# Gated attention with per-head states padded to 128 rows, a gate product over 128 rows, and level products of both halves placed together

## What is computed

```python
q = g_q.reshape(B, S, 4, 64) * 64 ** -0.5;  k = g_k...;  v = g_v.reshape(B, S, 4, 128)
log_a = log_sigmoid(g_a @ w_gate_up + b_gate) / 16       # g_a has 16 columns
# over chunks:
o_inter = einsum('bhcd,bhde->bhce', q * exp(b), state)   # b: running sum of log_a
o_intra = (q k^T with decay, causal) @ v
state = exp(b_last) * state + einsum('bhcd,bhce->bhde', k * exp(b_last - b), v)
```

## Time and profile before

| | us |
|---|---|
| median of 3 runs | 4049.37 (4048.47 to 4050.02) |
| span of the profiled execution | 4047.2 |
| PE busy | 4001.6 |
| DVE busy | 2201.4 |
| ACT busy | 1474.3 |
| POOL busy | 107.8 |
| GLA of layer 0 (gate to last norm product), from the span's start | 173 to 388 |
| GLA of layer 1 | 1430 to 1644 |

### The profile page before, as it was taken

How to read it: one execution, slowest core, us unless ns; L and a number is a source line. 1 busy time by engine, 2 the same in 40 slices (tenths; PEclk the granted TensorE clock), 3 DMA queues, 4 the chain that set the end, 5 groups by cost and what they waited for, 6 DMA issues and landing times.

```text
span 4047.2 us, 47426 instructions
## 1 busy us (share of the span) xinstructions
PE 4001.6 (99%) x18802; PEld 3076.8 (76%) x18802; DVE 2201.4 (54%) x3449; ACT 1474.3 (36%) x2422; POOL 107.8 (3%) x172
## 2 busy tenths in 40 slices
PE   9999999999999999999999999999999999999998
PEld 6777657888888877656888888777777777887786
DVE  7877677434434655566634334543546363646664
ACT  5434464211212433555412122333434343324533
POOL 2000000000000000000000000000000000000000
PEclk9999999999999999999999999999999999999999
DMA  7534101333332221201222221231111111116542
GB/s 263 193 109 141 40 11 32 99 94 104 94 99 83 90 67 48 76 6 37 63 88 89 78 68 47 73 110 47 37 47 44 40 47 63 42 54 227 187 160 80
DMA packets 99622, 342.13 MB, mean 85 GB/s; under 512 B 11016, under 2 KB 12072, under 8 KB 98250
## 3 DMA queue, kind: packets, MB, share of 16 engines
q1 hardware_dynamic: 78522, 258.87, 19.7%
q0 software_dynamic: 20880, 80.23, 6.3%
HBM read 304.45 MB, written 34.60 MB: 84 GB/s over the span
## 4 chain that ended last, share of the span: by engine, by line
PE 88%; DVE 7%; ACT 3%; issue 2%; DMA 0%; SPq 0%; DVEq 0%; POOL 0%; ACTq 0%
PE PS L1307 35%; PE PS L1289 20%; PE PS L2395 4%; PE PS L2254 3%; PE PS L3301 2%; PE PS L3365 2%; PE PS L2164 2%; PE PS L1007 1%; PE PS L1272 1%; PE PS L1692 1%; PE PS L1972 1%; PE PS L2685 1%; PE PS L2132 1%; PE PS L2712 1%; PE PS L2698 1%
## 5 line engine op out<-in xcount | busy, mean ns | idle before, releaser
L640 ACT ACTIVATE WH<-raw 128x1024 fp32r<-128x1024 f32 x314 | 330.4, 1052 | 676.0 <-PE PS L1307 443.8
L1289 PE MATMUL PS<-hi,WH 128*128 128x512 f32 x1248 | 524.0, 420 | 0.4 <-DVE WL L651 0.2
L1307 PE MATMUL PS<-hi,WL 128*128 128x512 f32 x1312 | 516.8, 394 | 0.0
L1307 PE MATMUL PS<-lo,WH 128*128 128x512 f32 x1312 | 514.3, 392 | 0.0
L1307 PE MATMUL PS<-hi,WH 128*128 128x512 f32 x1312 | 511.6, 390 | 1.2 <-DVE WL L651 0.7
L1289 PE MATMUL PS<-hi,WL 128*128 128x512 f32 x1248 | 491.0, 393 | 0.0
L1289 PE MATMUL PS<-lo,WH 128*128 128x512 f32 x1248 | 488.2, 391 | 0.0
L651 DVE TENSOR_TENSOR WL<-raw,WH 128x1024 fp32r<-128x1024 f32 x274 | 335.0, 1222 | 127.7 <-ACT WH L640 127.6
L1307 PE MATMUL PS<-ah,WL 128*128 128x512 f32 x768 | 302.6, 394 | 0.0
L1307 PE MATMUL PS<-al,WH 128*128 128x512 f32 x768 | 301.1, 392 | 0.0
L1307 PE MATMUL PS<-ah,WH 128*128 128x512 f32 x768 | 299.2, 390 | 0.0
(11 more groups left out here) (484 smaller groups left out, 6927.7 us busy)
## 6 DMA issues: line engine op xcount, KB each, us to landing
adab<-in_w_ada POOLq DMA_DIRECT2D x120, 512.0 KB, 4.6
raw<-in_win SPq DMA_DIRECT2D x104, 512.0 KB, 3.6
raw<-in_down SPq DMA_DIRECT2D x80, 512.0 KB, 3.6
raw<-in_up SPq DMA_DIRECT2D x64, 512.0 KB, 3.6
raw<-in_dft SPq DMA_DIRECT2D x24, 512.0 KB, 4.1
sp_x<-X SPq DMA_DIRECT2D x24, 512.0 KB, 6.2
X<-sp_x SPq DMA_DIRECT2D x24, 512.0 KB, 4.9
raw<-in_wout SPq DMA_DIRECT2D x24, 512.0 KB, 3.7
```

Source lines behind the costliest of these rows:

```text
L640: act.activation(PLACES[PLACE[j]][0], raw[:, j % 2, :], ACT.Copy).then_inc(*W_HI.next(j))
L1289: mm = pe.matmul(bank[b + hf], w[:, k, :], r[:, k, HALF[hf]], start=k == 0 and w is wh and r is hi, stop=k == 7 and w is wl)
L1307: mm = pe.matmul(bank[b + hf], w[:, k, :], r[:, k, HALF[hf]], start=k == 0 and w is wh and r is hi, stop=k == 7 and w is wl)
```

## The change

It does four things.

1. The gate product runs over all 128 rows of `wg` and `misc`. So `wg` is cleared as a whole by POOL before SP loads its 16 rows; SP's load now waits for POOL's clearing, and this for what the load waited for.
2. The states of the two heads of a pair lie in two tiles, `st` and a part of `mq` (its second tile, not yet written then), each with the other head's 64 rows zero. POOL clears these rows once in a layer. The state product runs over 128 rows: both heads' queries against a state whose other half is zero.
3. Because `mq` is lent, the evacuation of input tile 3 (the last in order) waits for the last output product of the pair 1.
4. The two halves of a level are planned 0.01 us apart, not 0.9.

```diff
@@ Memory
+            self.states = [self.st, self.mq[:, 1, 0:7 * P].rearrange("p (c b) -> p c b", c=7)]
@@ win_act
+                    elif hf == 0 and n == 3:
+                        act.wait_ge(*GL_PE["out", l, 1, 1, 1])
@@ gla_sp, gla_pool
             yield win_at(l, 1)
-            sp.wait_ge(*NO_DVE["low", l, 0, 7])
+            sp.wait_ge(*GL_POOL["gate rows", l])
             sp.dma_start(m.wg[64:80, :], D["w_gate_up"][l]).then_inc(*GL_WG.next(l, by=16))
 
         def gla_pool(pool, l):
+            yield win_at(l, 1)
+            pool.wait_ge(*NO_DVE["low", l, 0, 7])
+            pool.memset(m.wg[:, :], 0.0).then_inc(*GL_POOL.next("gate rows", l))
...
                 pool.memset(ATT[:, :, :, :], 0.0).then_inc(*GL_POOL.next("cleared", l, pr))
+                if pr == 0:
+                    for hd in range(2):
+                        pool.wait_ge(*GL_POOL.now())
+                        pool.memset(m.states[hd][64 - 64 * hd:128 - 64 * hd, :, :], 0.0).then_inc(*GL_POOL.next("other rows", l, hd))
@@ gla_decays_pe
-                    pe.matmul(bank[3 + hf], m.wg[64:80, pr * P:(pr + 1) * P], m.misc[64:80, HALF[hf]], start=True,
+                    pe.matmul(bank[3 + hf], m.wg[:, pr * P:(pr + 1) * P], m.misc[:, HALF[hf]], start=True,
                               stop=True).then_inc(*GL_PE.next("gate", l, pr, hf))
@@ gla_states_dve
+                            st = m.states[hd]
                             if ch == 0:
-                                step = dve.tensor_copy(m.st[r, 0, :], PS[r, 2, off:off + P])
+                                step = dve.tensor_copy(st[r, 0, :], PS[r, 2, off:off + P])
@@ gla_levels_pe
-                        yield level_at(l, pr, lv) + (2.8 if pr else 1.5) + 0.9 * g4
+                        yield level_at(l, pr, lv) + (2.8 if pr else 1.5) + 0.01 * g4
@@ gla_outputs_pe
+                            if pr == 0:
+                                pe.wait_ge(*GL_POOL["other rows", l, 1])
...
-                                mm = pe.matmul(PS[:, b, x * P:(x + 1) * P], m.st[r, ch - 1, :],
-                                               m.qd[r, ch * P:(ch + 1) * P], start=False, stop=True)
+                                mm = pe.matmul(PS[:, b, x * P:(x + 1) * P], m.states[hd][:, ch - 1, :],
+                                               m.qd[:, ch * P:(ch + 1) * P], start=False, stop=True)
```

More of the change, by code:

```diff
@@ L1620, in gla_states_dve @@
                             off = x * 256 + hd * P
+                            st = m.states[hd]
                             if ch == 0:
-                                step = dve.tensor_copy(m.st[r, 0, :], PS[r, 2, off:off + P])
+                                step = dve.tensor_copy(st[r, 0, :], PS[r, 2, off:off + P])
                             else:
-                                step = dve.scalar_tensor_tensor(out=m.st[r, ch, :], in0=m.st[r, ch - 1, :],
+                                step = dve.scalar_tensor_tensor(out=st[r, ch, :], in0=st[r, ch - 1, :],
                                                                 scalar=m.el[r, ch:ch + 1], in1=PS[r, 2, off:off + P],
@@ L1720, in gla_outputs_pe @@
                 for hd in range(2):
-                    r = slice(64 * hd, 64 * hd + 64)
                     vcol = (2 * pr + hd) * P
```

## The result

| | median us | runs | profiled span |
|---|---|---|---|
| before | 4049.69 | 4048.47 to 4050.81 | 4047.2 |
| after | 4027.78 | 4025.65 to 4030.78 | 4026.6 |
| forecast | 4020.1 | range 4013.5 to 4027.0 | 4017.9 |

The row of before takes in a fourth run, so its median is 0.3 us above the one given ahead of the prediction. The ratio is 0.9947, 95% interval 0.9935 to 0.9958: faster, by 21.9 us where 29.3 was forecast, and 0.8 us outside the range. Of the gross of 34.4 us, 20.6 are left in the profiled span.

What follows compares the result with a forecast made beforehand. The prediction took the length of PE's own program to bound the kernel. Gains of 21.7 + 3.1 + 9.6 = 34.4 us less 5.1 of new waits left 29.3, so 4020.1 us; forecast 4016 to 4023.5, wider range 4013.5 to 4027.

Steps and rivals of the forecast that it cites:

- State, gate and level terms: Gains in PE's own program: state products 21.7 us, gate products 3.1, level halves together 9.6; gross 34.4.
- Rival 2: State products: only the changes of mode go, not the doubled time within a product; 11 us instead of 21.7, 4031 us; 5 in 100.
- joints of levels: Level products: running both halves of a level together gains 8.4 us over 24 joints plus 1.2 for QK, 9.6 us.
- Level operands: Level stages: PE waits longer for DVE's operands (L1604), forecast loss 3.6 us.
- level 0 of pair 0: Both layers: level 7's value transposes come 0.9 us later, so PE waits 1.0 us here, twice, 2.0 in all.
- level 1 of pair 1: Both layers: PE waits already and DVE has no gap, so 0.35 us won earlier is waited again; 0.7 in all.
- allowance: 0.9 us for L1604 waits in layer 0's other levels and behind the gate products, between 0 and 2.9.
- Rival 4: Whole kernel: nothing is late, so the whole 34.4 us is gained, 4015 us; 10 in 100.
- rival 1: Level stages: DVE keeps the pace, so the joints bring nothing; gain 22.1 to 25 us, 4024 to 4027 us; 12 in 100.
- The dots behind the outputs of layer 0: Modulation dots, paced by their loads, hold DVE's next step after layer 0's outputs; loss 1.5 us, between 0 and 2.5.
- Costed at nothing: Clearing wg and the other rows on POOL, the wait before evacuating tile 3, and DVE's state steps: no loss.
- rival 3: POOL's clearing of wg comes late and holds SP's loads; 33 us lost against 29.3 won, 4053 us; 2 in 100.

Runs made afterwards that it cites:

- e6: Kernel before, each output group doing all 64-row state products first, then all 128-row score products, which overwrite the states' part; 4036.60 us, ratio 0.9970.
- e4: Kernel after, with DVE's copy of the second four transposed value chunks moved behind the operands of level 0, both layers; 4024.22 us, ratio 0.9938.
- e1: Kernel after, with the two halves of a level planned 0.9 us apart again, leaving only the padding to 128 rows; 4032.07 us, ratio 0.9956.
- e2: Kernel before, with the two halves of a level planned 0.01 us apart and nothing else; 4046.09 us, ratio 0.9990.
- e7: Kernel after, with layer 0's last two modulation dots taken by DVE behind the output norm's steps, no transfer moved; 4022.32 us, ratio 0.9934.
- e3: Kernel after, with layer 0's reload of six X blocks waiting for the modulation dot before the last one; 4022.06 us, ratio 0.9934.
- e8: Kernel after, with layer 0's last two dots late, the value copy behind level 0's operands, and ACT evacuating values earlier; 4020.02 us, ratio 0.9928.
- e5: Kernel after, with layer 0's X reload late, the value copy behind level 0's operands, and ACT evacuating values earlier; 4018.92 us, ratio 0.9924.
- e10: Kernel after, with all four edits: X reload late, last two dots late, value copy late, value evacuation early; 4020.42 us, ratio 0.9925.
- e11: Kernel after, with layer 0's last two dots late and the value copy late, the evacuation where it was; 4020.84 us, ratio 0.9928.

## Why the prediction was wrong, point by point

- **State, gate and level terms (34.4 gross):** the pieces right, and for the right reason: e6 shows the price of a change of rows with no row padded. Rival 2 falls, a group takes 2.49 us and not 3.2. All 34.4 us were not there: the joints of levels brought about 1.2 us less than their price per piece. The Trainium skill (TensorE: Matmul & The Clock Gate, step 4 of Part 2) gives a drain as about 128 cycles, an estimate of 0.053 us a change; the runs show 0.2, and the measurement decides.
- **Level operands (3.6: level 0 of pair 0 twice 1.0, level 1 of pair 1 0.7, allowance 0.9):** right, 3.6. The two waits of 1.00 us stand where they were put, and e4 shows that their cause, the copy that waits for transposed values, was the named one. Rival 4, in which nothing was late, falls. So does rival 1, in which the joints bring nothing: they bring 4.3 us (e1 against after) and 4.0 (e2). That its 4024 to 4027 lies near the measured time is chance.
- **The dots behind the outputs of layer 0 (1.5, at most 2.5):** the step that failed, with 5.3 us. The prediction held the dots against the gain of the output groups just before (5.6 us; by its own prices 2 x (1.55 + 1.16) = 5.4, and the marks give 5.4), and let them go on at the pace that their loads had before. The first half was sound. The dots are tied to PE up to the last picks and had moved with it: the lead is 7.6 us there, and the dots start 6.4 to 7.1 us earlier up to the one at 362.08. Had the last two kept the 6.6 us of that one, L1767 would have been held for 13.0 (PE's lead) - 6.6 - 4.1 (DVE's room before, 376.0 to 380.09) = 2.3 us, an estimate from these rows, inside the 2.5 that the prediction allowed for this. The second half failed, the pace: the load of `VT` and two blocks of X follow PE, came 12.8 us earlier and ran beside the last two loads of dots, of which the first took some 8.8 us instead of 4.5. So the last dot came only 3.7 us earlier, and 13.0 - 3.7 - 4.1 = 5.2 us is what L1767 was held; the timeline has 372.44 - 367.05 = 5.4. The prediction thought of the loads only as landing earlier. e7 (the dots moved, nothing lost between the marks) shows that the dots held the norm, and e3 (a dot's load in 3.9 us instead of 8.2, and 2.0 us lost in place of 5.3) that other transfers slow their loads; that it was `VT` and these two blocks of X is read from the times of issue, no run moves them alone.
- **Half clock:** not in the sum. The one in layer 1, behind a wait of 1.00 us that the change made, cost 1.6 us, more than the wait itself. The one in layer 0 fell where PE would have waited anyway.
- **Costed at nothing:** clearing `wg` and the other rows cost PE nothing (0.53 us on POOL for `wg`, where 0.23 was worked out); SP's load of `wg` starts at 155.44, 1.6 us later than before, of which 1.0 is the slower opening stage, so SP was not held and rival 3 falls. Not seen: the wait for ACT's evacuation of values at L1377, 0.5 us longer in each layer. e1 has it and e2 has not, so it comes with the padding, and of that only the gate's gain lies ahead of it.
- **The range** took in the dots' 2.5 and nothing for the clock. With the measured 5.3 in place of 1.5, 0.5 twice for L1377 and one half clock of 1.6, the forecast's 4020.1 becomes 4026.5, and the 1.2 us missing at the joints make it 4027.7. That e8 and e5 come near the forecast's own figure, 4020.1, is in part luck: they have undone 2.0 of the 3.6 us at the levels and the whole loss at the dots, which the forecast had counted as lost. The best versions found are e5 (4018.9), e8, e10 and e11 (4020.0 to 4020.8), which their runs do not tell apart. By the medians they are 28 to 31 us faster than before and 7 to 9 faster than after; against before their ratios are 0.9924 to 0.9928, with intervals from 0.9911 to 0.9941, that of after is 0.9947 (0.9935 to 0.9958), so the intervals still touch.
- **Open:** why the joints bring 1.2 us less than their pieces, and what decides whether a short wait brings the lower clock.

## What to carry to other kernels

Count the changes of rows on TensorE, not the products: each costs about 0.2 us here, and padding with zeros or grouping by rows takes them away. When an engine gets faster, so do the transfers that follow it, and they can come to run beside loads that another engine's steps wait for. Put the issues of both queues side by side at their new times before you price a load-paced step, and hold that step against the bound engine's lead since the two were last tied. And order the queue so that what the bound engine waits for stands ahead of what waits for a transfer.

## What was not expected of the hardware

A wait of PE between 0.8 and 4 us is followed by the lower clock sometimes, and not always at the same wait. In e6 a wait of 2.39 us at the third norm product of pair 1 in layer 0, and one of 2.23 at the fourth, leave the clock at 1.00, while one of 2.13 us at the third product brings it to 0.57 in e4 (rows of e6, then of e4):

```profile
377.43 1.13 PE L1747 MATMUL PS<-X,const 128*128 128x512 f32 x2 [2.39 <-ACT X L1800]
```

```profile
300.00:400.00 100.00, 94.83 (x560) 72.64 (x558) 71.68 (x123) 40.19 (x66) 6.33 (x12) 1.00 0.44 143
```

```profile
371.42 1.94 PE L1757 MATMUL PS<-X,const 128*128 128x512 f32 x2 [2.13 <-ACT X L1810]
```

```profile
371.00:375.00 4.00, 3.58 (x7) 2.19 (x8) 1.30 (x2) 3.97 (x8) 0.00 (x0) 0.57 0.00 0
```

In e3 and e7 the wait of 1.0 us at level 0 in layer 1 stands as it does in after, and the clock behind it stays at 1.00. In e7 the lower clock came behind a wait of 0.81 us instead, where after kept the full clock behind a wait of 0.79 at the same product (303.29):

```profile
302.36 2.00 PE L1703 MATMUL PS<-X 64*128 64x64 f32 x32 [0.81 <-DVE X L1614]
```

```profile
305.00:310.00 5.00, 5.00 (x17) 3.87 (x15) 4.99 (x10) 1.12 (x2) 0.40 (x1) 0.68 0.33 105
```

So in a kernel that PE bounds, a wait of a microsecond can be followed by a loss of some 1.6 us more, unless PE would have waited in that stretch anyway. Since it falls in different places, it may well be part of the scatter between runs of one kernel; the runs without a trace do not show it.
